# The last expert pair gets weight slots of its own, and the gate and up work of the last two pairs goes ahead of their down work

## The chip, the core and the metric

One core of a Trainium2 chip runs the whole program. The engines named here are PE (TensorE, the matrix engine), DVE (VectorE), ACT (ScalarE), POOL (GpSimd), and SP (SyncE), which does nothing but issue transfers and wait. The transfers themselves run on sixteen DMA engines. The metric is the device time of one execution in microseconds, of which each comparison takes the median of several.

## What is computed

The program is one layer of a transformer-like model for 640 tokens (512 latent ones and 128 of a prompt) of width 1024: two token mixers (retention and differential attention) with their projections, then a mixture of experts, then a final norm. All of it is float32. The change touches only the mixture of experts and the final norm:

```
# hf: the 640 normalised tokens; 4 groups of 8 experts, 32 in all
p_grp = softmax(hf @ rgw + rgb);          g_idx = top-1 group of each token
e_top, e_idx = top-2 experts in that group
w = p_top * e_top / sum(e_top)
a = silu(hf @ wg[e]) * (hf @ wu[e])       # wg, wu: 1024 x 256 of each expert
y = (a * w) @ wd[e], summed over e        # wd: 256 x 1024 of each expert
x = x + g2 * y
out = rmsnorm(x, final_norm_g)
```

Each expert has 1 MB of gate, 1 MB of up and 1 MB of down weights, 96 MB for all of them, and each is read once.

## The kernel before, in words

The 32 experts are worked through in 16 pairs (PAIRS), 0 to 15. Each expert has a block of 64 rows (tokens sent to it), and a pair fills the 128 partitions. Tokens beyond 64 for an expert would go through an overflow part that does not run on this data.

Work of one pair p, with par = p % 2:

- POOL gathers the pair's 128 token rows from DRAM into xg[par] (rows_in, L1913), and PE transposes them through PSUM banks 0 and 1 (gathered, L1037); ACT copies them to xgT[par] (L1317).
- PE multiplies them with the gate and up weights of both experts into bank 2 + par (gate_up, 16 matmuls, 32 instructions in the trace, L1043).
- ACT takes the tanh (L1322), DVE forms silu times up times the routing weight (L1779 and L1784).
- PE transposes the result into bank 4 (hidden, L1049), ACT copies it to act_aT[par] (L1326), and PE multiplies it with the down weights into banks 5 and 6 (down, L1056).
- ACT and DVE each copy half of the result to y_out[par] (L1332 and L1792), and POOL scatters the rows to y_dram in DRAM (rows_out, L1919).

PE's order is written out by hand in `pair` (L1065): gate_up of p, transpose of the rows of p + 1, hidden of p, down of p. ACT's order is in `whole`, DVE's in its own `pair`, POOL's is rows_in(p + 2) and then rows_out(p). Each engine waits on semaphores that count what the others have done: pe_gu counts finished gate_up products, pe_dn finished down products, ld_gu[slot] and ld_dn[slot] the landed weights, y_a and y_d the copied results, st_y[par] the scattered rows.

Weights live in six slots, one expert each: w_gu[0..5] and w_dn[0..5]. The first three pairs take slots 0 and 1, 2 and 3, 4 and 5. From pair 3 on only slots 0 to 3 are used, in turns: odd pairs slots 0 and 1, even pairs slots 2 and 3; slots 4 and 5 stay unused. SP refills a pair of slots in next_weights(p, e, slot): it waits until gate_up of pair p is done, issues the four gate and up loads (L652), waits until down of pair p is done, and issues the two down loads (L655). next_weights(0), (1), (3), (4), ... (13) run in this order, the last for the weights of pair 15. Between next_weights(1) and next_weights(3), behind a wait for three finished down products, SP issues three row loads for the final stage into tiles where slot 5 was: g2_rows (two, L753) and fin_row (L754), 0.5 MB each, a row of DRAM repeated to all 128 partitions.

After the last pair SP waits for all scattered rows (L762) and loads them back, five tiles of 128 tokens twice, since each token has two experts: y1[t] and y2[t] (L779 and L780). Tile 0 is summed by DVE (L1826), tiles 1 to 4 by PE, which adds both with an identity matrix into a pair of banks each (L1120 and L1121, semaphore pe_sum). DVE then does three more steps for each tile (L1831, L1832, L1834), ACT and POOL the norm, and SP the store.

## Time and profile before

| | us |
|---|---|
| median of 3 runs | 1346.71 (1345.1 to 1347.92) |
| the profiled execution, its time | 1347.75 |
| the profiled execution, its span | 1345.9 |
| granted TensorE clock over the span | 0.95 |
| busy over the span: PE | 1145.1 (85%) |
| DVE, ACT, POOL | 499.0, 402.0, 86.4 |
| DMA over the span | 222.28 MB, mean 165 GB/s |

All times on a line of the trace are microseconds from the first instruction. The expert stage begins at about 1045 and its last scatter lands at 1311.29; the rest is the read-back, the sum and the final norm. In the timeline each row is a start, a duration and an instruction; what stands in brackets is the time the engine sat idle before it and what released it. A row of a transfer on SP or POOL is its issue and not the transfer; how long that took is in the view of the DMA issues.

### The profile page before, as it was taken

Reading aid. Unit: us, or ns where it says so; the run is one execution under the profiler, and the core shown is the slowest. Engines: PE = TensorE matmul, PEld = TensorE weight load, DVE = VectorE, ACT = ScalarE, POOL = GpSimd, SP = SyncE. Lnnn points to the kernel's source line nnn. Section 1 sums busy time; section 2 is a strip of 40 time slices with the busy share of each in tenths; the row PEclk is TensorE's granted clock in tenths of the full one; section 3 lists DMA queues with packets and bytes.
Section 4 is the critical chain, followed back from the end, with each engine's and each line's share of the span. In section 5 each row is a group of like instructions: output and inputs, shape, how many; then the busy total and the mean of one; then the engine's idle time right before and its main releaser. Section 6 shows DMA issues by size and latency. Waiting matters only on the chain. (4 is left out here: it accounts for less than half of the span.)

```text
span 1345.9 us, 19161 instructions
## 1 busy us (share of the span) xinstructions
PE 1145.1 (85%) x8001; PEld 921.6 (68%) x8001; DVE 499.0 (37%) x892; ACT 402.0 (30%) x862; POOL 86.4 (6%) x103
## 2 busy tenths in 40 slices
PE   2699999999988999999988887898873888777765
PEld 0488899889987888889977776798872433222222
DVE  0521116554434344433435555546556111111115
ACT  2522222212244454542245544313120121111113
POOL 0000000211000000000000000000000111111001
PEclk9799999989999999999999999899985799999987
DMA  8655631211311312232221110924128499999925
GB/s 301 228 179 193 209 108 38 90 40 32 108 58 48 95 59 91 64 108 73 71 93 50 48 52 22 413 71 137 49 96 357 176 400 420 421 421 421 417 116 234
DMA packets 90273, 222.28 MB, mean 165 GB/s; under 512 B 9881, under 2 KB 64962, under 8 KB 74706
## 3 DMA queue, kind: packets, MB, share of 16 engines
q1 hardware_dynamic: 85586, 210.66, 42.6%
q0 software_dynamic: 4608, 10.49, 2.1%
q8 instruction: 59, 0.97, 0.3%
q14 instruction: 20, 0.16, 0.0%
HBM read 206.41 MB, written 21.00 MB: 169 GB/s over the span
## 5 line engine op out<-in xcount | busy, mean ns | idle before, releaser
L840 PE MATMUL ps<-w_high,h_high 128*128 128x256 f32 x1280 | 370.5, 289 | 10.1 <-DVE arena L1506 5.2
L840 PE MATMUL ps<-w_low,h_high 128*128 128x256 f32 x1280 | 363.9, 284 | 0.0
L840 PE MATMUL ps<-w_high,h_low 128*128 128x256 f32 x1280 | 363.7, 284 | 0.0
L840 PEld LDWEIGHTS ps<-w_high,h_high 128*128 128x128 f32 x1280 | 247.3, 193 | 24.6 <-ACT arena L1231 10.1
L840 PEld LDWEIGHTS ps<-w_low,h_high 128*128 128x128 f32 x1280 | 247.4, 193 | 0.2
L840 PEld LDWEIGHTS ps<-w_high,h_low 128*128 128x128 f32 x1280 | 247.2, 193 | 0.0
L1580 DVE TENSOR_TENSOR w_low<-w_loaded,w_high 128x2048 fp32r<-128x2048 f32 x44 | 100.8, 2291 | 174.4 <-ACT w_high L1259 174.3
L1043 PE MATMUL ps<-arena 128*64 128x512 f32 x512 | 124.1, 641 | 26.3 <-DMA arena<-in_moe_w_up 22.5
L1043 PEld LDWEIGHTS ps<-arena 128*64 128x64 f32 x512 | 40.2, 147 | 108.7 <-issue 108.7
L1231 ACT COPY arena<-ps 128x256 f32<-128x256 f32 x100 | 37.2, 372 | 249.7 <-PE ps L840 249.7
L1259 ACT CAST w_high<-w_loaded 128x2048 fp32r<-128x2048 f32 x44 | 84.0, 1908 | 57.4 <-DMA w_loaded<-in_w_o 32.9
L1286 ACT ACTIVATE arena<-ps,neg_mx 128x768 f32<-128x768 f32 (+1 forms) x80 | 62.8, 790 | 106.3 <-DVE neg_mx L1646 106.3
L1056 PE MATMUL ps<-arena 128*64 128x512 f32 x256 | 60.2, 612 | 9.8 <-ACT arena L1326 9.8
L1779 DVE SCALAR_TENSOR_TENSOR arena<-arena,ps 128x256 f32<-128x256 f32 x16 | 6.7, 421 | 145.9 <-ACT arena L1322 145.9
L1015 PE MATMUL ps<-arena 128*128 128x128 f32 x384 | 49.3, 278 | 13.3 <-ACT arena L1293 13.3
L1644 DVE TENSOR_REDUCE mx<-ps 128x1 f32<-128x768 f32 (+1 forms) x40 | 32.9, 822 | 71.5 <-PE ps L985 71.5
L1015 PEld LDWEIGHTS ps<-arena 128*128 128x128 f32 x384 | 45.5, 192 | 16.1 <-ACT arena L1293 16.1
L985 PE MATMUL ps<-arena 64*128 64x256 f32 (+2 forms) x288 | 53.9, 488 | 2.5 <-ACT arena L1180 1.5
L873 PE MATMUL ps<-const,arena 128*128 128x128 f32 x256 | 40.4, 286 | 13.2 <-POOL arena L1893 3.5
L840 PE MATMUL ps<-w_high,m_high 128*128 128x256 f32 x160 | 48.0, 300 | 2.5 <-DVE m_low L1548 0.8
L1322 ACT ACTIVATE arena<-ps 128x256 f32<-128x256 f32 x16 | 6.1, 384 | 139.2 <-PE ps L1043 139.2
L840 PE MATMUL ps<-w_high,od_high 128*128 128x256 f32 x160 | 46.2, 289 | 1.7 <-DVE od_whole L1477 0.9
(253 smaller groups left out, 1715.4 us busy)
## 6 DMA issues: line engine op xcount, KB each, us to landing
w_loaded<-in_w_in SPq DMA_DIRECT2D x32, 1024.0 KB, 5.7
arena<-in_moe_w_gate SPq DMA_DIRECT2D x32, 1024.0 KB, 13.3
arena<-in_moe_w_up SPq DMA_DIRECT2D x32, 1024.0 KB, 19.7
arena<-in_moe_w_down SPq DMA_DIRECT2D x32, 1024.0 KB, 20.9
arena<-in_w_ada SPq DMA_DIRECT2D x24, 1024.0 KB, 5.9
gates<-arena SPq DMA_DIRECT2D x40, 128.0 KB, 1.7
arena<-y_rows SPq DMA_DIRECT2D x10, 512.0 KB, 7.5
arena<-in_x_sample SPq DMA_DIRECT2D x8, 512.0 KB, 11.2
```

The costliest lines, as they stand in the source:

```text
L840: mm = pe.matmul(out[:, 0:N256], x[:, t, k * P:(k + 1) * P], w[i % 2][:, k, :], start=(k == 0 and j == 0), stop=(k == KC - 1 and j == 2))
L873: mm = pe.transpose(out[:, k * P:(k + 1) * P], src[k], ident)
L985: mm = pe.matmul(score[c][:, lo:hi], qT[h % 2][r, t * P:(t + 1) * P], keys, start=True, stop=True, skip_group_check=True)
L1015: mm = pe.matmul(pv_out, mixedT[s % 2][:, k * P:(k + 1) * P], v, start=(k == 0), stop=(k == 5))
L1043: mm = pe.matmul(B(bank_at)[BLK * i:BLK * (i + 1), :].rearrange("p (g f) -> p g f", g=2), xgT[slot][:, k, BLK * i:BLK * (i + 1)], w_gu[e0 ...
L1056: mm = pe.matmul(B(5 + n)[BLK * i:BLK * (i + 1), :], act_aT[slot][:, k, BLK * i:BLK * (i + 1)], w_dn[e0 + i][:, k, n * N512:(n + 1) * N512 ...
L1231: free(act.copy(dst[:, t, c0:c0 + N256], src), n)
L1259: act.copy(w_hi[i % 2][:], w_raw[i % 2]).then_inc(w_rounded, 1)
L1286: act.activation(probs[:, c, 0:n], score[c][:, 0:n], ACT.Exp, bias=neg_mx[:, s % 2, c:c + 1], scale=DH ** -0.5, accum_out=den[:, s % 2, c: ...
L1580: dve.tensor_tensor(w_lo[i % 2][:], w_raw[i % 2], w_hi[i % 2][:].bitcast(F32), ALU.subtract).then_inc(w_split, 1)
L1644: dve.tensor_reduce(mx[:, 0:1], score[0][:, 0:n], AXX, ALU.max)
L1779: ins = dve.scalar_tensor_tensor(out=act_s[:, par, :], in0=act_t[:, par, :], scalar=1.0, in1=src[:, 0:FF], op0=ALU.add, op1=ALU.mult)
```

## The change

SP refills slots 0 and 1 for pair 13 as before, and then issues the gate and up loads of pairs 14 and 15 together, when gate_up of pair 12 is done: pair 14 into slots 2 and 3, pair 15 into slots 4 and 5. When down of pair 12 is done it issues the four down loads of both. The three row loads of the final stage follow, behind a wait for gate_up of pair 14, and go to where slot 3 was. PE leaves its loop after pair 12, does pair 13, and then: gate_up 14, transpose of the rows of 15, hidden 14, gate_up 15, down 14, hidden 15, down 15. ACT and DVE follow this order for the last two pairs. y2 has another place, an unused tile (fin_t) is gone, and in the final sum DVE adds tiles 0 and 1 and PE tiles 2 to 4.

```diff
--- before.py
+++ after.py
@@ -198,9 +198,8 @@
         act_t, act_s = tiles(134, 2, FF), tiles(136, 2, FF)
         act_a, act_aT = tiles(194, 2, FF), [at(196 + i, 2 * P).rearrange("p (k n) -> p k n", k=2) for i in range(2)]
 
-        g2_rows, fin_row = tiles(118, 2, D), at(126, D)
-        fin_t = tiles(162, 2, D)
-        y1, y2 = tiles(28, NT, D), tiles(48, NT, D)
+        g2_rows, fin_row = tiles(138, 2, D), at(146, D)
+        y1, y2 = tiles(28, NT, D), tiles(86, NT, D)
 
         scr_at = [178]
 
@@ -747,16 +746,23 @@
 
             next_weights(0, 6, 0)
             next_weights(1, 8, 2)
-            sp.wait_ge(pe_dn, 3)
-
+            with sp.Fori(0, (PAIRS - 8) // 2) as i:
+                next_weights(2 * i + 3, 4 * i + 10, 0)
+                next_weights(2 * i + 4, 4 * i + 12, 2)
+            next_weights(PAIRS - 5, NE - 6, 0)
+
+            sp.wait_ge(pe_gu, PAIRS - 3)
+            for e, slot in ((NE - 4, 2), (NE - 3, 3), (NE - 2, 4), (NE - 1, 5)):
+                load_gate_up(e, slot)
+            sp.wait_ge(pe_dn, PAIRS - 3)
+            for e, slot in ((NE - 4, 2), (NE - 3, 3), (NE - 2, 4), (NE - 1, 5)):
+                load_down(e, slot)
+
+            sp.wait_ge(pe_gu, PAIRS - 1)
             for i in range(2):
                 sp.dma_start(g2_rows[:, i, :], mod_dram[i, 5 * D:6 * D].partition_broadcast(P)).then_inc(ld_fin, 16)
             sp.dma_start(fin_row, a["final_norm_g"].partition_broadcast(P)).then_inc(ld_fin, 16)
 
-            with sp.Fori(0, (PAIRS - 6) // 2) as i:
-                next_weights(2 * i + 3, 4 * i + 10, 0)
-                next_weights(2 * i + 4, 4 * i + 12, 2)
-            next_weights(PAIRS - 3, NE - 2, 0)
             n_over = sp.value_load(n_ov[0:1, 0:1], min_val=0, max_val=OVER)
             for par in range(2):
                 sp.wait_ge(st_y[par], 16 * PAIRS // 2)
@@ -1087,10 +1093,38 @@
             pair(0, 0, 0, 0, 0, first=True)
             pair(1, 1, 2, 0, 0)
             pair(2, 0, 4, 1, 0)
-            with pe.Fori(0, (PAIRS - 4) // 2) as i:
+            with pe.Fori(0, (PAIRS - 6) // 2) as i:
                 pair(2 * i + 3, 1, 0, i + 1, i + 1)
                 pair(2 * i + 4, 0, 2, i + 2, i + 1)
-            pair(PAIRS - 1, 1, 0, PAIRS // 2 - 1, PAIRS // 2 - 1, last=True)
+            h = PAIRS // 2 - 1
+            pair(PAIRS - 3, 1, 0, h - 1, h - 1)
+
+            a_p, b_p = PAIRS - 2, PAIRS - 1
+            for i in (2, 3):
+                pe.wait_ge(ld_gu[i], 32 * h)
+            pe.wait_ge(xt_read, a_p + 1)
+            gate_up(0, 2, 2).then_inc(pe_gu, 1)
+            pair_gathered(b_p, 1, h)
+            pe.wait_ge(gu_act, a_p + 1)
+            hidden(0).then_inc(pe_aT, 1)
+            for i in (4, 5):
+                pe.wait_ge(ld_gu[i], 64)
+            pe.wait_ge(xt_read, b_p + 1)
+            gate_up(1, 4, 3).then_inc(pe_gu, 1)
+            pe.wait_ge(aT_read, a_p + 1)
+            for i in (2, 3):
+                pe.wait_ge(ld_dn[i], 16 * h)
+            pe.wait_ge(y_a, a_p)
+            pe.wait_ge(y_d, a_p)
+            down(0, 2).then_inc(pe_dn, 1)
+            pe.wait_ge(gu_act, b_p + 1)
+            hidden(1).then_inc(pe_aT, 1)
+            pe.wait_ge(aT_read, b_p + 1)
+            for i in (4, 5):
+                pe.wait_ge(ld_dn[i], 32)
+            pe.wait_ge(y_a, b_p)
+            pe.wait_ge(y_d, b_p)
+            down(1, 4).then_inc(pe_dn, 1)
 
             n_over = pe.value_load(n_ov[0:1, 0:1], min_val=0, max_val=OVER)
             pe.wait_ge(y_a, PAIRS)
@@ -1113,12 +1147,12 @@
             with pe.Else():
                 pe.nop()
 
-            for t in range(1, NT):
+            for t in range(2, NT):
                 pe.wait_ge(ld_y[t], 32)
                 for n in range(2):
                     c = slice(n * N512, (n + 1) * N512)
-                    pe.matmul(B(2 * t - 2 + n), ident, y1[:, t, c], start=True, stop=False)
-                    mm = pe.matmul(B(2 * t - 2 + n), ident, y2[:, t, c], start=False, stop=True)
+                    pe.matmul(B(2 * t - 4 + n), ident, y1[:, t, c], start=True, stop=False)
+                    mm = pe.matmul(B(2 * t - 4 + n), ident, y2[:, t, c], start=False, stop=True)
                 mm.then_inc(pe_sum, 1)
 
         @block.scalar
@@ -1345,8 +1379,13 @@
                 for par in range(2):
                     whole(2 * i + par, par, i)
             h = PAIRS // 2 - 1
-            whole(2 * h, 0, h)
-            whole(2 * h + 1, 1, h, last=True)
+            pair_gate(2 * h, 0)
+            pair(2 * h + 1, 1)
+            pair_hidden(2 * h, 0)
+            pair_gate(2 * h + 1, 1)
+            pair_rows(2 * h, 0, h)
+            pair_hidden(2 * h + 1, 1)
+            pair_rows(2 * h + 1, 1, h)
             n_over = act.value_load(n_ov[0:1, 0:1], min_val=0, max_val=OVER)
             act.wait_ge(st_y[0], 16 * PAIRS // 2)
             act.wait_ge(st_y[1], 16 * PAIRS // 2)
@@ -1791,16 +1830,23 @@
                     dve.wait_ge(st_y[par], 16 * turn)
                 dve.tensor_copy(y_out[:, par, N512:D], B(6)).then_inc(y_d, 1)
 
-            def pair(p, par, turn, first=False):
+            def pair_act(p, par):
                 dve.wait_ge(gu_tanh, p + 1)
                 silu_up(B(2 + par), par, (gu_half, p + 1), gu_act, p)
+
+            def pair(p, par, turn, first=False):
+                pair_act(p, par)
                 pair_rows(p, par, turn, first=first)
 
             pair(0, 0, 0, first=True)
             pair(1, 1, 0, first=True)
-            with dve.Fori(1, PAIRS // 2) as i:
+            with dve.Fori(1, PAIRS // 2 - 1) as i:
                 for par in range(2):
                     pair(2 * i + par, par, i)
+            for par in range(2):
+                pair_act(PAIRS - 2 + par, par)
+            for par in range(2):
+                pair_rows(PAIRS - 2 + par, par, PAIRS // 2 - 1)
             n_over = dve.value_load(n_ov[0:1, 0:1], min_val=0, max_val=OVER)
             dve.wait_ge(st_y[0], 16 * PAIRS // 2)
             dve.wait_ge(st_y[1], 16 * PAIRS // 2)
@@ -1821,13 +1867,13 @@
 
             dve.wait_ge(ld_fin, 16 * 3)
             for t in range(NT):
-                if t == 0:
-                    dve.wait_ge(ld_y[0], 32)
-                    link(dve.tensor_tensor(y1[:, 0, :], y1[:, 0, :], y2[:, 0, :], ALU.add))
-                    both = y1[:, 0, :]
+                if t < 2:
+                    dve.wait_ge(ld_y[t], 32)
+                    link(dve.tensor_tensor(y1[:, t, :], y1[:, t, :], y2[:, t, :], ALU.add))
+                    both = y1[:, t, :]
                 else:
-                    dve.wait_ge(pe_sum, t)
-                    both = psf[:, (2 * t - 2) * N512:2 * t * N512]
+                    dve.wait_ge(pe_sum, t - 1)
+                    both = psf[:, (2 * t - 4) * N512:(2 * t - 2) * N512]
                 link(dve.tensor_tensor(y1[:, t, :], both, g2_rows[:, 1 if t == PT else 0, :], ALU.mult))
                 dve.tensor_tensor(x1[:, t, :], x1[:, t, :], y1[:, t, :], ALU.add).then_inc(x2_ready, 1)
                 dve.wait_ge(x2_ready, t + 1)
```

## Rows read from the trace of the kernel before

**Rows 1.** Page, forty slices of the span: GB/s that the DMA engines moved

```profile
GB/s 301 228 179 193 209 108 38 90 40 32 108 58 48 95 59 91 64 108 73 71 93 50 48 52 22 413 71 137 49 96 357 176 400 420 421 421 421 417 116 234
```

**Rows 2.** Windows: span, busy time by engine (instructions), PE clock, DMA share, GB/s

```profile
1099.00:1104.00 5.00, 4.73 (x26) 1.86 (x22) 0.68 (x2) 0.62 (x2) 0.80 (x1) 1.00 0.98 297
...
1124.00:1283.00 159.00, 123.03 (x558) 44.67 (x554) 17.05 (x29) 23.05 (x48) 19.24 (x19) 0.96 1.01 420
...
1283.00:1296.00 13.00, 10.05 (x40) 3.49 (x40) 0.69 (x1) 1.10 (x3) 1.00 (x1) 0.87 0.31 129
```

**Rows 3.** Chain of waits from 1200 us: start, length, what

```profile
1248.17 25.52 DMA arena<-in_moe_w_up
...
1287.32 2.49 issue
1289.80 8.80 PE ps L1043 x32
...
1308.08 3.21 DMA y_rows<-arena,to_idx
...
1312.87 6.17 DMA arena<-y_rows
```

**Rows 4.** Timeline of SP's queue: start, length, line, transfer issued

```profile
1252.90 0.81 SPq L655 DMA_DIRECT2D arena<-in_moe_w_down  x2
...
1266.96 0.53 SPq L652 DMA_DIRECT2D arena<-in_moe_w_up  x1
...
1272.33 0.80 SPq L655 DMA_DIRECT2D arena<-in_moe_w_down  x2
```

**Rows 5.** DMA issues, us to landing: loads issued at 1253.3, 1266.96 and 1272.7

```profile
arena<-in_moe_w_down SPq DMA_DIRECT2D x1, 1024.0 KB, 25.5
...
arena<-in_moe_w_up SPq DMA_DIRECT2D x1, 1024.0 KB, 22.7
...
arena<-in_moe_w_down SPq DMA_DIRECT2D x1, 1024.0 KB, 22.6
```

**Rows 6.** Timeline of PE from 1256 to 1307 us

```profile
1256.81 8.78 PE L1043 MATMUL ps<-arena 128*64 128x512 f32 x32 [3.95 <-DMA arena<-in_moe_w_up]
...
1273.92 7.09 PE L1043 MATMUL ps<-arena 128*64 128x512 f32 x32 [1.63 <-DMA arena<-in_moe_w_up]
...
1282.76 0.44 PE L1049 MATMUL ps<-const,arena 128*128 128x128 f32 x2 [0.73 <-DVE arena L1784]
...
1283.66 3.65 PE L1056 MATMUL ps<-arena 128*64 128x512 f32 x16 [0.46 <-ACT arena L1326]
...
1301.23 5.35 PE L1056 MATMUL ps<-arena 128*64 128x512 f32 x16 [0.46 <-ACT arena L1326]
```

**Rows 7.** DMA issues: loads of pair 3 (first two) and pair 5, median

```profile
arena<-in_moe_w_up SPq DMA_DIRECT2D x2, 1024.0 KB, 9.9
...
arena<-in_moe_w_down SPq DMA_DIRECT2D x2, 1024.0 KB, 11.9
...
arena<-in_moe_w_up SPq DMA_DIRECT2D x2, 1024.0 KB, 12.1
...
arena<-in_moe_w_down SPq DMA_DIRECT2D x2, 1024.0 KB, 14.5
```

**Rows 8.** Timeline of ACT, PE and DVE at the end

```profile
1306.63 0.58 ACT L1332 COPY arena<-ps 128x512 f32<-128x512 f32 x1 [5.45 <-PE ps L1056]
...
1319.08 2.07 PE L1120 MATMUL ps<-arena,const 128*128 128x512 f32 x2 [12.51 <-DMA arena<-y_rows]
...
1325.69 1.02 PE L1120 MATMUL ps<-arena,const 128*128 128x512 f32 x2
...
1325.89 1.22 DVE L1831 TENSOR_TENSOR arena<-ps,arena 128x1024 f32<-128x1024 f32 x1 [4.32 <-PE ps L1121]
```

**Rows 9.** DMA issues: fin_row load at 1096.72, and scatter of pair 13 at 1273.81

```profile
arena<-in_final_norm_g SPq DMA_DIRECT2D x1, 512.0 KB, 11.1
...
y_rows<-arena,to_idx POOLq DMA_INDIRECT x1, 8.2
```

## What the change does to the time: the prediction

> **What bounds the kernel now.** Read the page's forty slices first, then the chain of waits, then the transfers one by one, and the PE rows last. The slices of the expert stage, from the thirty-third to the thirty-eighth, all move some 420 GB/s [rows 1], and the windows say the same in another form: from 1124 to 1283 us the sixteen DMA engines are busy throughout at 420 GB/s [rows 2]. PE, which does the arithmetic, is not full there. So between 1124 and 1283 us the expert stage is a stream of weights, 6.3 MB for each of the sixteen pairs of experts, and what PE does in between is hidden. What is not hidden is the end. The chain of waits shows it [rows 3]: the second up load of pair 14 lands at 1248.17 + 25.52 = 1273.69; later the gate and up products of pair 15 run from 1289.80 for 8.80 us; the last scatter of rows starts at 1308.08 and takes 3.21 us; and the read-back of rows that PE's first sum waits for ends at 1319.04. After 1283 us the DMA engines fall idle one by one, 129 GB/s on the mean until 1296 [rows 2].
>
> Two things about the start of pair 15. The chain puts the 2.49 us ahead of it down to "issue" [rows 3], which names no releaser. The transfers do: the last up load is issued at 1266.96 [rows 4] and takes 22.7 us [rows 5], so it lands at 1289.66, and PE starts 0.14 us later. That load is what PE waits for, not the way out of the loop. Second, these products run for 8.8 us, and the same 32 instructions of pair 14 took 7.09 [rows 6]: part of them is at the lower of the two granted clocks (1.2 and 2.4 GHz); the mean of 1283 to 1296 is 0.87 [rows 2].
>
> **The change part by part.** I write times on the clock of the kernel before, and take off the shift of part 1 at the end.
>
> 1. The three row loads (1.5 MB for the final stage) go from the third pair to the end. The last of them leaves at 1096.72 [rows 9], and the window from 1099 to 1104, which holds most of their bytes, moves only 297 GB/s at a busy share of 0.98 [rows 2]. Without them the engines would be nearly empty when the weights of pair 5 are issued at about 1103, as they were when those of pair 3 were issued. The price is the difference between these two: the up loads take 12.1 us instead of 9.9, the down loads 14.5 instead of 11.9 [rows 7], so 2.2 and 2.6 us. From then on the stream has no gap, so what it gains there it keeps to its end. I take the mean, 2.4 us. The bounds are 0 (the queue would stand still for as long anyway) and 3.7 us (their whole 1.57 MB at 420 GB/s); 2.4 is nearest to the direct comparison. That PE keeps its own pace in the first pairs costs nothing, because each load of the stream is issued long before the engines come to it.
>
> 2. The gate and up loads of pair 15 are issued beside those of pair 14 and ahead of all four down loads. Nothing of the volume changes, only the order. The two down loads of pair 14 no longer lie ahead of the last up load. They are issued in one go from 1252.90 [rows 4]; the second, issued about 1253.3, takes 25.5 us [rows 5] and lands at 1278.8, and the up load ahead of it landed at 1273.69. So two down loads cost the slowest engine 5.1 us. The last up load lands at 1289.66 - 5.1 = 1284.56. Bounds: 0, if the order inside the engines is not the order of issue (a rival below), and 5.1.
>
> 3. PE does gate and up of pair 14, transposes its hidden rows, does gate and up of pair 15, and then both down products. Gate and up of pair 14 still start at 1273.92; the hidden transposes of pair 14 are over at 1282.76 + 0.44 = 1283.2 [rows 6]. PE then waits for 1284.56, so 1.4 us, and starts at about 1284.8 instead of 1289.8. Ahead of products that ran at the higher clock throughout, 1.63 us of idle time was seen; ahead of those of 8.78 us it was 3.95 and 2.49 [rows 3, 6]. 1.4 is on the side of the fast ones, so I take 7.1 us: until 1291.9. Down of pair 14 follows at once, since its weights landed at 1289.7 at the latest (now behind the last up load, 1284.56 + 5.1), and takes 3.65 us [rows 6]: 1295.55. The activation of pair 15 (ScalarE, then VectorE) is hidden beside it. Then the hidden transposes of pair 15, and 0.90 us from their start to the next down product as before [rows 6], plus ScalarE's copy of pair 14's rows, which now is ahead of the hidden copy on its queue: 0.58 us [rows 8], of which 0.4 lies beside the transposes. That makes 1.1 us; the last down product runs from 1296.65 to 1300.3. Its weights: the last down load is issued at about 1272.7 [rows 4], takes 22.6 us [rows 5] and lands at 1295.3, in either order, since the total is the same: 1.3 us to spare. Before, this point was 1301.23 + 5.35 = 1306.6 [rows 6]. That is 6.3 us: 5.0 from the earlier start, 1.7 from the clock of the gate and up products, and 0.4 lost on what is behind them (8.4 us against 8.0).
>
> 4. The row loads themselves now wait for the gate and up products of pair 14 (1281 us). Behind that wait on SP's queue is only the read-back, and it comes 30 us later. The last of the three took 11.1 us from issue to landing [rows 9], part of it behind weights. On the slowest engine they now begin behind the last down load, at 1295.3: by their bytes they are in 3.7 us later, at 1299.0, and at the worst 11.1 us later, at 1306.4. VectorE wants them only when the first rows are read back, a few microseconds behind that. The last scatter is issued 1.5 us behind the last down product (1306.6 to 1308.08), so at 1301.8. By their bytes the loads are over then, and I take nothing for it; bounds 0 and 5.0 us, the difference between a scatter on busy engines, 8.2 us [rows 9], and the last one, 3.21 [rows 3].
>
> 5. The final sum: VectorE adds tile 1 itself, and PE begins with tile 2. VectorE stood 4.32 us ahead of tile 1's product [rows 8], from 1321.57; four steps of 1.22 us now follow there, to 1326.5. PE's sum of tile 2 can start when its rows are in, 1.05 MB at 420 GB/s or 2.5 us behind tile 1's 1319.04: 1321.5. Tile 1's sum took from 1319.08 to 1325.69, 6.6 us, mostly at the lower of the two granted clocks (1.2 GHz; its first instructions take 2.07 us, and the same of the next tile 1.02 at 2.4 GHz [rows 8]). So tile 2 is ready for VectorE at 1328.3, and three tiles of three steps follow, 3.66 us each: 1339.3 instead of 1325.89 + 4 x 3.66 = 1340.5. Some of the 1.2 is lost between loads; I take 0.9. Bounds: 0, and 3.0, if PE has its full clock from the start and VectorE's 1326.5 is what counts.
>
> Other edits move nothing: the new places of the row tiles and of y2 are free when they are written, and the loops of SP, ScalarE and VectorE do the same pairs in the same order up to pair 13.
>
> Sum: 2.4 + 6.3 + 0.9 = 9.6 us. The profiled execution has a span of 1345.9 and a time of 1347.75; it would become 1338.15. It is 1.0 above the median of 1346.71, so the median becomes 1337.1.
>
> **Rivals.**
> A. The lower clock stays. If the granted clock falls in the new, shorter waits too, gate and up of pair 15 keep 8.8 us (+1.7) and one down product 5.35 instead of 3.65 us (+1.7) [rows 6]: gain 6.2, 1340.5 us. For it speaks that 1.4 us is not far from the smallest wait that had a slow group behind it (2.49); against it that 1.63 had none.
> B. Part 1 gives nothing, because the stream stands still by as much ahead of pair 5: gain 7.2, 1339.5 us.
> C. The moved rows are in the way of the last scatter, which takes 8.2 us: gain 4.6, 1342.1 us. Against it: by their bytes they are in 2.8 us before its start. For it: so few bytes were moved while they ran before [rows 2].
> D. The edit does not do what it says: the last up load lands no earlier, since the slowest engine keeps its place. Then the products of pair 15 start as now, at the lower clock, and the path behind them is 0.4 us longer: gain 2.4 - 0.4 + 0.9 = 2.9, 1343.8 us.
> E. Slower: transfers in flight share the engines. Twelve loads of 1 MB are now issued within 10 us; if they move side by side, the up loads of pair 14 come with the last of them at 1295.3 - 2.4 = 1292.9, and four products stand behind that: 9.3 us from the start of pair 14's gate and up to the end of its transposes, then 7.1, 3.65, 1.1 and 3.65, in sum 24.8, so 1317.7 against 1306.6. With the 0.9 of part 5 that is 10.2 us more, 1356.9. It decides from an arrival at 1306.6 + 0.9 - 24.8 = 1282.7, where I expect 1271.3. Against it: the up loads of pair 14 and 15 land in the order of their issue, 16.0 us apart, with 6.3 MB between them at 420 GB/s (15.0 us) [rows 3, 4, 5]; a fair share would have pulled them together.
> On E the Trainium skill has a rule: "DMA: Bandwidth & Descriptors", section "Queues, rings and completion order", says that each DMA engine takes the descriptors of one issuer's ring in order and only takes turns between rings. All these loads are SyncE's, so by that rule E gives nothing and the sum stays at 9.6; the 16.0 us above agree with it. The same section says that completion is not in order across the engines, which is what D would need.
>
> **How the numbers follow.** Chances: forecast 0.58, A 0.15, B 0.10, C 0.08, D 0.05, E 0.04. The likeliest case gives 1337.1. Its low side is all of part 1 (3.7) and part 5 (3.0) with 6.3: 13.0 us, 1333.7. A and B together give 1346.7 - 3.8 = 1342.9; the range goes up to 1342.4, which takes in A, B and C one at a time and leaves out D, E and most of the overlaps. About 2.7 us, 0.2%, is what a measurement of this kernel can tell from no change. Faster by more than that: 0.90 (forecast, A, B, C, a third of D, less the overlaps); within 0.2%: 0.06; slower: 0.04 (E).
>
> **What would show it.** Part 1: the last up load of pair 14 lands at about 1271.3 and not 1273.7, and few bytes move between 1100 and 1104. Part 2: the last up load lands 13 us behind it at most, not 16. Part 3: gate and up of pair 15 take 7.1 us, and four products follow with under 2 us of idle time between any two. Part 4: the last scatter takes about 3.2 us. Part 5: VectorE waits some 2 us ahead of tile 2 and hardly behind it. The prediction is wrong if gate and up of pair 14 start later than now, or if the last scatter is issued behind 1302 us.

## The result, and the profile after

The changed kernel takes 1339.26 us (median of 9 executions, 1335.72 to 1343.83), the kernel before 1346.14 in the same session: a ratio of 0.995, 95% interval 0.9933 to 0.9967, or 6.9 us faster. The forecast was 1337.1 us with a range of 1333.7 to 1342.4. Two more comparisons of the same pair gave 0.996 (0.9944 to 0.9976) and 0.9934 (0.9922 to 0.9947), so the gain is about 7 us (mean ratio 0.9948) where the sum said 9.6. No ratio in this document counts one execution of 2270.06 us (the changed kernel with early row loads too; its other 11 took 1337.76 to 1344.55).

The page after: span, clock granted to TensorE in forty slices (tenths), and GB/s of the DMA engines.

```profile
span 1339.0 us, 19112 instructions
...
PEclk9799999989999999999999999899985699999897
...
GB/s 304 220 173 195 211 104 53 78 57 32 103 64 47 88 63 66 86 66 111 84 91 48 32 37 40 349 123 101 117 48 343 136 398 379 422 421 422 421 271 237
```

The stream is as full as before, 421 GB/s up to the thirty-eighth slice. The last two slices differ: 271 and 237 GB/s where [rows 1] has 116 and 234. The end of the weights and the read-back have come closer together.

Windows of the kernel after: span, busy time by engine (PE, PEld, DVE, ACT, POOL), PE clock, DMA share, GB/s. In this execution the expert stage began 4.4 us later than in that of [rows 2], so the window of 1099 to 1104 us there is 1103.4 to 1108.4 here; the others stand at the same times as there.

```profile
1103.40:1108.40 5.00, 3.96 (x22) 1.63 (x18) 1.08 (x2) 1.72 (x4) 0.00 (x0) 1.00 0.53 138
...
1104.00:1124.00 20.00, 17.21 (x80) 7.22 (x78) 2.86 (x5) 4.25 (x9) 2.03 (x2) 0.91 0.89 347
1124.00:1283.00 159.00, 125.66 (x566) 46.48 (x566) 16.67 (x28) 22.35 (x46) 19.26 (x19) 0.96 1.02 421
1283.00:1296.00 13.00, 12.13 (x62) 5.22 (x60) 2.17 (x4) 2.19 (x5) 0.00 (x0) 1.00 0.74 274
```

The stretch that held the row loads before (share 0.98 at 297 GB/s [rows 2]) now has gaps, share 0.53 at 138 GB/s. The 20 us from 1104, which take in most of it, have 0.89. From 1124 to 1283 nothing has changed (1.02 at 421). Between 1283 and 1296 there are 274 GB/s where there were 129: the down loads of pair 14 and 15 and the rows now lie there.

PE at the end, as [rows 6]; in brackets the idle time before and its releaser.

```profile
1275.30 8.78 PE L1049 MATMUL ps<-arena 128*64 128x512 f32 x32 [2.04 <-issue]
...
1286.41 7.09 PE L1049 MATMUL ps<-arena 128*64 128x512 f32 x32 [0.26 <-DMA arena<-in_moe_w_up]
1293.30 3.63 PE L1062 MATMUL ps<-arena 128*64 128x512 f32 x16
1296.86 0.44 PE L1055 MATMUL ps<-const,arena 128*128 128x128 f32 x2
1297.88 3.65 PE L1062 MATMUL ps<-arena 128*64 128x512 f32 x16 [0.58 <-ACT arena L1360]
```

The gate and up products of pair 15 start 11.1 us behind those of pair 14, where [rows 6] and the chain of [rows 3] have 15.9 (1273.92 to 1289.80). They take 7.09 us, and those of pair 14 take 8.78: the other way round than before.

How the transfers came in order: SP's issues (start, length), and below them the us to landing of the up loads issued at 1251.08 and 1255.34, as [rows 4, 5].

```profile
1251.08 0.43 SPq L651 DMA_DIRECT2D arena<-in_moe_w_up  x1
1251.55 0.43 SPq L651 DMA_DIRECT2D arena<-in_moe_w_gate  x1
1252.03 1.09 SPq L651 DMA_DIRECT2D arena<-in_moe_w_up  x1
1253.16 2.14 SPq L651 DMA_DIRECT2D arena<-in_moe_w_gate  x1
1255.34 2.14 SPq L651 DMA_DIRECT2D arena<-in_moe_w_up  x1
```

```profile
arena<-in_moe_w_up SPq DMA_DIRECT2D x1, 1024.0 KB, 24.1
...
arena<-in_moe_w_up SPq DMA_DIRECT2D x1, 1024.0 KB, 31.0
```

The last up load of pair 14 lands at 1251.08 + 24.1 = 1275.2, the last one of pair 15 at 1255.34 + 31.0 = 1286.3: 11.1 us apart, 16.0 before. The chain of waits from there on (start, length, what) is as [rows 3]:

```profile
1255.34 30.98 DMA arena<-in_moe_w_up
...
1286.41 7.09 PE ps L1049 x32
...
1293.49 3.45 PE ps L1062 x16
...
1297.88 3.68 PE ps L1062 x16
...
1303.03 3.22 DMA y_rows<-arena,to_idx
...
1309.27 7.91 DMA arena<-y_rows
...
1317.23 2.08 PE ps L1154 x2
```

The last scatter takes 3.22 us, as before (3.21). Pair 15's products still wait for their last up load, and everything behind them is one unbroken chain.

VectorE in the final sum, as [rows 8]: tile 1, added by VectorE itself, and the first step on tile 2, which PE adds.

```profile
1311.70 1.23 DVE L1872 TENSOR_TENSOR arena<-arena 128x1024 f32<-128x1024 f32 x1 [9.43 <-DMA arena<-y_rows]
...
1322.64 1.23 DVE L1877 TENSOR_TENSOR arena<-ps,arena 128x1024 f32<-128x1024 f32 x1 [1.02 <-PE ps L1155]
```

It stood 4.32 us ahead of PE's first sum in [rows 8], and now 1.02.

**Two whole profiles are not a measurement.** The span fell from 1345.9 to 1339.0, which fits the medians, but by a sum of two unlike things: the part ahead of the expert pairs, which the change does not touch, came out 4.3 us longer, and the expert stage and the end 11.2 us shorter. For that reason I cut all profiles at the same events. Each row below is one profiled execution. The columns: start of the stage's first product on PE (1039.87 us in the kernel before), which ends what the expectations call the part ahead of the slot table; from the end of pair 0's gate and up products to the start of pair 14's (the stream); from there to the start of pair 15's; from there to the end of the last down product, in brackets the lengths of pair 15's gate/up and down products; from the issue of the read-back to the end; and all behind the first column (the whole stage). Between the last down product and the issue of the read-back there are always 5.0 to 5.6 us. What the stage has beyond these columns is pair 0's own gate and up products and what leads to them, 22 to 23.5 us.

| kernel | ahead | stream | 14 to 15 | 15 to last down | read-back to end | whole stage |
|---|---|---|---|---|---|---|
| before | 1039.9 | 210.6 | 15.9 | 16.8 (8.8, 5.3) | 34.4 | 306.0 |
| before, again | 1040.3 | 210.1 | 16.0 | 15.1 (8.8, 3.7) | 33.1 | 301.3 |
| after | 1044.2 | 208.8 | 11.1 | 15.1 (7.1, 3.7) | 32.5 | 294.8 |
| after, again | 1045.8 | 208.6 | 11.1 | 16.8 (8.8, 3.7) | 34.0 | 298.8 |
| after, third | 1046.1 | 208.4 | 11.1 | 16.8 (8.8, 3.7) | 32.0 | 296.7 |
| rows late only | 1039.8 | 208.8 | 16.0 | 13.4 (7.1, 3.7) | 34.9 | 300.2 |
| after, rows early too | 1041.1 | 209.8 | 11.1 | 15.1 (7.1, 3.7) | 33.6 | 297.3 |
| final sum only | 1044.1 | 210.4 | 15.9 | 15.1 (8.8, 3.7) | 32.9 | 301.5 |
| new loads, old product order | 1042.9 | 208.4 | 21.2 | 13.3 (7.0, 3.7) | 32.3 | 303.5 |
| new product order, down loads between | 1039.5 | 208.5 | 16.3 | 17.7 (9.6, 3.7) | 33.8 | 303.5 |
| after, three slot pairs | 1043.3 | 204.9 | 12.2 | 15.1 (7.1, 3.7) | 32.7 | 293.4 |
| the same, again | 1044.2 | 205.0 | 11.1 | 16.8 (8.8, 3.7) | 33.3 | 294.0 |
| before, six early row loads | 1040.2 | 215.5 | 16.0 | 15.0 (7.0, 5.3) | 35.4 | 310.2 |
| three slot pairs, old order | 1039.7 | 204.9 | 16.4 | 13.4 (7.1, 3.7) | 32.6 | 294.6 |

The columns "stream" and "14 to 15" repeat within 0.5 us for one kernel (once 1.1, in the kernel with three slot pairs). The others depend on the granted clock and don't.

### The profile page after: what moved, and what is told of

It reads as the page before. It is cut to its first block and busy times, and to the rows that moved or that the text cites. A ratio compares the mean times of both kernels' runs of the same rounds, so it can differ in the third digit from the quotient of the medians.

```text
span 1339.0 us, 19112 instructions
## 1 busy us (share of the span) xinstructions
PE 1143.7 (85%) x7993; PEld 927.6 (69%) x7993; DVE 500.3 (37%) x893; ACT 402.4 (30%) x862; POOL 88.5 (7%) x103
## 5 line engine op out<-in xcount | busy, mean ns | idle before, releaser
L846 PE MATMUL ps<-w_high,h_high 128*128 128x256 f32 x1280 | 371.2, 290 | 10.1 <-DVE arena L1545 5.2
L846 PEld LDWEIGHTS ps<-w_high,h_high 128*128 128x128 f32 x1280 | 248.0, 194 | 24.6 <-ACT arena L1265 10.1
L1293 ACT CAST w_high<-w_loaded 128x2048 fp32r<-128x2048 f32 x44 | 84.0, 1908 | 58.2 <-DMA w_loaded<-in_w_o 33.6
L1021 PE MATMUL ps<-arena 128*128 128x128 f32 x384 | 49.3, 278 | 13.3 <-ACT arena L1327 13.3
L1683 DVE TENSOR_REDUCE mx<-ps 128x1 f32<-128x768 f32 (+1 forms) x40 | 32.9, 822 | 71.5 <-PE ps L991 71.3
L846 PE MATMUL ps<-w_high,o_high 128*128 128x256 f32 x160 | 46.9, 293 | 0.8 <-DVE o_low L1587 0.8
```

Of the source, the lines that this page charges most:

```text
L846: mm = pe.matmul(out[:, 0:N256], x[:, t, k * P:(k + 1) * P], w[i % 2][:, k, :], start=(k == 0 and j == 0), stop=(k == KC - 1 and j == 2))
L1021: mm = pe.matmul(pv_out, mixedT[s % 2][:, k * P:(k + 1) * P], v, start=(k == 0), stop=(k == 5))
L1293: act.copy(w_hi[i % 2][:], w_raw[i % 2]).then_inc(w_rounded, 1)
L1683: dve.tensor_reduce(mx[:, 0:1], score[0][:, 0:n], AXX, ALU.max)
```

## The experiments

All but the second are timed against the kernel before on the same chip; the ratios have their 95% interval. They were timed in three sets, each on another chip: the pair again, part 1 alone and the changed kernel with early rows in the first; the final sum, the two halves of the new order and the three slot pairs in the second; the rest in the third. Kernels of different sets are compared by their ratios. None of them changes what is computed. The theory is the sum of the prediction; its rivals are A to E.

**The pair again.** No edit.

> The changed kernel once more. In its first profile the part from the first product of the slot table to the end of the span is 294.8 us (306.0 in the kernel before, so 11.3 less), but the part ahead of it, which the change does not touch, is 1044.2 us against 1039.9. Theory 1 (the 4.4 us ahead are chance: the granted clock of the dense part falls at other places in every execution): the part ahead lies between 1037 and 1043 here and is not tied to the kernel, and the part behind is 294 to 296 again; the ratio over five rounds is 0.992 to 0.994. Theory 2 (the changed program is slower ahead of the experts, by where its code or data lie): the part ahead is 1043 to 1045 again, and the ratio is 0.995.

> The kernel before once more, for a second look at its two parts. Theory 1 (chance): the part ahead of the slot table is anywhere from 1037 to 1044, the part behind it 305 to 307. Theory 2 (tied to the program): 1039 to 1041 again.

Measured: 0.996 (0.9944 to 0.9976), 1340.5 us against 1345.03. The profiled execution of the changed kernel took 1346.39 us, 5.9 above its own median, and that of the kernel before 1343.48. Neither theory had the numbers: the part behind the slot table is 298.8 us in the one and 301.3 in the other, the part ahead 1045.8 and 1040.3. Pair 15's gate and up products took 8.8 us in the changed kernel this time, and the last down product 3.7 in the kernel before. So both the 7.09 above and the 5.35 of [rows 6] come out otherwise in another execution of the same kernel, and the prediction had compared a good outcome with a bad one. PE in this execution of the changed kernel, pairs 14 and 15:

```profile
1277.45 7.09 PE L1049 MATMUL ps<-arena 128*64 128x512 f32 x32 [0.95 <-issue]
...
1288.56 8.78 PE L1049 MATMUL ps<-arena 128*64 128x512 f32 x32 [1.96 <-DMA arena<-in_moe_w_up]
```

Here the products of pair 14 take 7.09 us, and PE then waits 1.96 us for the last up load; above they took 8.78 us, which left a wait of 0.26.

**Part 1 alone.** The row loads of the kernel before behind its last loads of weights:

```diff
-            sp.wait_ge(pe_dn, 3)
-            for i in range(2):
-                sp.dma_start(g2_rows[:, i, :], ...)
-            sp.dma_start(fin_row, ...)
...
             next_weights(PAIRS - 3, NE - 2, 0)
+            sp.wait_ge(pe_gu, PAIRS - 1)
+            for i in range(2):
+                sp.dma_start(g2_rows[:, i, :], ...)
+            sp.dma_start(fin_row, ...)
```

> The kernel before with one edit: the three row loads are issued behind the loads of the last pair, when the gate and up products of pair 14 are done, and not in the third pair. My theory: this alone is worth the shift of the weight stream, 2.4 to 3.0 us: the part behind the slot table is 303 to 303.6 instead of 306.0, the gate and up products of pairs 8 to 14 each begin 3 us earlier against the slot table, and the last scatter is not slower (3.2 us). Rival (the weight stream stands still as long in any case): 306.0. Rival (the rows are in the way at the end): over 306.

Measured: 0.9968 (0.9953 to 0.9982), 1341.6 us. Its stream is 208.8 us, against 210.1 to 210.6. The part behind the slot table is 300.2 us, less than expected, as the last group of gate and up products came out fast. The whole change had 0.996 (0.9944 to 0.9976) in the same set: by these executions alone part 1 gained as much as all parts together (means 1341.7 and 1340.9 us, a difference of 0.8 with a 95% interval of 2.2 to either side). The window of the row loads (columns as above), and PE's last products:

```profile
1099.00:1104.00 5.00, 3.75 (x22) 1.60 (x18) 1.08 (x2) 1.83 (x4) 0.00 (x0) 1.00 0.54 139
```

```profile
1286.72 7.09 PE L1042 MATMUL ps<-arena 128*64 128x512 f32 x32 [2.57 <-issue]
...
1296.44 3.65 PE L1055 MATMUL ps<-arena 128*64 128x512 f32 x16 [0.46 <-ACT arena L1325]
```

Share 0.54, as the changed kernel's 0.53: the engines stand still for 2.3 of 5 us there, so not all that the row loads took came back. The second fence shows gate and up of pair 15 at 7.09 us behind 2.57 us of idle time. In [rows 3] they had 8.80 behind 2.49. At such a length idle time ahead of the group does not tell its clock.

**Part 1 undone in the changed kernel, and doubled in the kernel before.** Three row loads of the same kind into free space, which nothing reads; once beside the late ones of the changed kernel, once beside the early ones of the kernel before (where it makes six):

```diff
+            for i in range(2):
+                sp.dma_start(more[:, i, :], mod_dram[i, 5 * D:6 * D].partition_broadcast(P))...
+            sp.dma_start(more[:, 2, :], a["final_norm_g"].partition_broadcast(P))...
```

> The changed kernel with three row loads more, issued in the third pair as before the change, into slot 5, whose weights come much later; the late ones stay. My theory: it gives back the shift of the stream, 2.4 to 3.0 us, and nothing else: 297.2 to 297.8 us behind the slot table instead of 294.8. Rival (the shift came from somewhere else, such as the first pair's products, which ran 1.0 us faster in the first profile after): 294.8 to 295.8.

> The kernel before with three row loads more beside the early ones, into a free slot. In the other runs the products of pair 14 begin 210.1 to 210.7 us behind the end of pair 0's gate and up products with the early row loads, 208.4 to 208.9 without, so 1.8 us for 1.57 MB, where their bytes alone are 3.7 us. My theory: they lie in a gap of the weight stream (about 3.2 us idle without them), which hides the rest, and once it is full every further byte costs in full: 4 to 5.5 us more, so 214 to 216, and a ratio to the kernel before of 1.003 to 1.004. Rival (the cost of a row load is simply 0.6 us): 212.

Measured: 0.9971 (0.9957 to 0.9984), and 1.002 (1.0006 to 1.0034). The edit shown is the second's; the first differs in the place and the name. The first has a stream of 209.8 us, 1.0 to 1.4 longer than the changed kernel's, and 297.3 us behind the slot table. The second has 215.5, so the second three cost 5.1 us where the first three cost 1.8. Over whole executions (1350.21 us against 1347.22) they cost 0.2%, 2.7 us, less than the expected 0.3 to 0.4% and with an interval that ends at 4.6 us. So the 5.1 of one profile may be too much. Window of the second:

```profile
1099.00:1104.00 5.00, 4.97 (x28) 1.92 (x24) 0.43 (x2) 0.38 (x1) 1.02 (x1) 1.00 1.02 305
```

At 305 GB/s the share is 1.02: while rows move the engines are fully busy and bring less. The first three loads cost only what sticks out of a gap that is there anyway; the second three, in this profile, cost all of their time (1.57 MB at 305 GB/s is 5.2 us).

**Part 5 alone.** The kernel before with the new final sum (VectorE adds tiles 0 and 1, PE tiles 2 to 4).

```diff
-                if t == 0:
+                if t < 2:
```

> The kernel before with the final sum alone changed: VectorE adds tiles 0 and 1, PE tiles 2 to 4. My theory: from the issue of the read-back to the end of the span it takes 0.9 us less than in the kernel before (34.4 and 33.1 us in its two profiles), so 32.2 to 33.5, and VectorE waits about 2 us ahead of tile 2. Rival: nothing, because PE's first sum is as late against its rows as before and VectorE waits for it all the same: 33.1 to 34.4. Over whole runs it is near what can be measured: ratio 0.998 to 1.000.

Measured: 0.999 (0.9976 to 1.0004), not to be told from 1. VectorE ahead of its first step on tile 2:

```profile
1329.17 1.23 DVE L1831 TENSOR_TENSOR arena<-ps,arena 128x1024 f32<-128x1024 f32 x1 [1.63 <-PE ps L1121]
```

Its wait is 1.63 us and not 4.32. In the table, the stretch from read-back to end is 34.4, 33.1, 34.9 and 35.4 us with the old sum (mean 34.5) and 32.0 to 34.0 in the ten with the new one (mean 33.0). That is about 1.5 us, less than the 2 us by which either varies, so the size stays rough.

**New loads, old order of products.** The changed kernel, but PE, ACT and DVE go through pairs 14 and 15 as before:

```diff
-            gate_up(0, 2, 2).then_inc(pe_gu, 1)
...
-            down(1, 4).then_inc(pe_dn, 1)
+            pair(PAIRS - 2, 0, 2, h, h - 1)
+            pair(PAIRS - 1, 1, 4, h, 1, last=True)
```

> The changed kernel's slots and loads, but PE, ScalarE and VectorE do pairs 14 and 15 in the old order (down of 14 ahead of gate and up of 15). My theory: the early up load is wasted, since the down load of pair 14 now lands at about 248 us behind the slot table and PE waits for it ahead of the products of pair 15; these start at 251 to 252 (242.2 and 242.8 changed, 249.9 and 248.2 before) and the last down product ends at 262 to 265 (257.4 and 259.6 changed; 266.7 and 263.3 before). Rival (the loads alone are what counts): products at 246 to 247, end at 258 to 260.

Measured: 1.0029 (1.0017 to 1.0041), 1348.73 us, slower than the kernel before. PE's products of pairs 14 and 15:

```profile
1274.54 9.88 PE L1049 MATMUL ps<-arena 128*64 128x512 f32 x32 [3.69 <-issue]
...
1290.68 5.21 PE L1062 MATMUL ps<-arena 128*64 128x512 f32 x16 [4.08 <-issue]
...
1295.71 7.05 PE L1049 MATMUL ps<-arena 128*64 128x512 f32 x32
...
1305.39 3.65 PE L1062 MATMUL ps<-arena 128*64 128x512 f32 x16 [0.46 <-ACT arena L1336]
```

Down of pair 14 (1290.68) waits 4.08 us. The trace names no releaser, but its weights are the loads that were moved back: the second of them is issued at 1258.91 and lands at 1290.48, 0.2 us ahead of the product. Gate and up of pair 15 stand behind it though their own weights landed at 1285.53, and start 21.2 us behind those of pair 14. They start 252.8 us behind the slot table and the last down product ends at 266.2, both about a microsecond later than the expectation had at most.

**New order of products, down loads of pair 14 between.** The changed kernel with the slots and the early issue kept, and only the order in the stream changed:

```diff
-            for e, slot in ((NE - 4, 2), (NE - 3, 3), (NE - 2, 4), (NE - 1, 5)):
+            for e, slot in ((NE - 4, 2), (NE - 3, 3)):
                 load_gate_up(e, slot)
             sp.wait_ge(pe_dn, PAIRS - 3)
-            for ...: load_down(e, slot)
+            for e, slot in ((NE - 4, 2), (NE - 3, 3)):
+                load_down(e, slot)
+            for e, slot in ((NE - 2, 4), (NE - 1, 5)):
+                load_gate_up(e, slot)
+            for e, slot in ((NE - 2, 4), (NE - 1, 5)):
+                load_down(e, slot)
```

> The changed kernel's slots and PE order, but the down loads of pair 14 are issued between the gate and up loads of 14 and those of 15. My theory: the place in the stream is the whole gain of the loads, 2 MB or 4.8 us of it: the products of pair 15 start 15.9 us behind those of pair 14 as before, at 247, and the last down product ends at about 262 us behind the slot table. Rival (it is the early issue into free slots that counts): 11.1 us behind, at 242, and the end at 257 to 260.

Measured: 1.0011 (0.9998 to 1.0025), 1347.14 us.

```profile
1270.24 8.78 PE L1053 MATMUL ps<-arena 128*64 128x512 f32 x32 [2.04 <-issue]
...
1286.55 9.63 PE L1053 MATMUL ps<-arena 128*64 128x512 f32 x32 [5.46 <-DMA arena<-in_moe_w_up]
...
1296.01 3.61 PE L1066 MATMUL ps<-arena 128*64 128x512 f32 x16
...
1300.57 3.65 PE L1066 MATMUL ps<-arena 128*64 128x512 f32 x16 [0.58 <-ACT arena L1364]
```

From 14 to 15 it is 16.3 us again, with 5.46 us of waiting for the up load; the products of pair 15 start 247.0 us behind the slot table, as expected, and the last down product ends at 264.7, later than the 262 expected, as those products were slow. Slots of its own and an earlier issue bring pair 15 nothing; two fewer loads ahead of it bring it 5 us. And the product order without the load order gives away again what parts 1 and 5 gain, since two down products and a slow gate and up stand at the end.

**The gap filled.** The changed kernel with all six slots used in turns throughout, the loads of pair p issued when pair p - 3 has let go of its slots; the loops of SP and PE are written out:

```diff
+            for p in range(3, PAIRS - 2):
+                next_weights(p - 3, 2 * p, 2 * (p % 3))
```

and the same with the old order of loads and products for the last two pairs.

> The changed kernel with all six slots in turns from pair 3 to 15 (the loads of a pair are issued when the gate and up products of the third pair ahead of it are done), loops of SP and PE written out. My theory: the weight stream loses its one gap, ahead of pair 5, where the engines now stand 3.2 us idle in sum between 1099 and 1124 us; the products of pair 14 start 205.5 to 206.5 us behind the end of pair 0's gate and up products (208.6 and 208.8 changed, 210.1 and 210.7 before), and the ratio to the kernel before is 0.992 to 0.994. Rival (nothing left: SP stands at its full queue, or the gap only moves): 208.5 and over, 0.995 or more.

> All six slots in turns and the late row loads, but the old order of loads and products for the last two pairs. My theory: it keeps the stream's gain (products of pair 14 at 205 us behind the end of pair 0's gate and up products), but pair 15 follows 16 us behind 14, and not 12; the last down product ends 4 to 5 us later than with the new order (255.5 behind the slot table), at 260. Rival (with more loads in flight the order no longer counts): 255 to 256.

Measured: 0.9932 (0.9915 to 0.995), 1336.86 us, and 0.9954 (0.9937 to 0.9971), 1340.38 us. Windows of the first:

```profile
1099.00:1104.00 5.00, 5.00 (x26) 1.63 (x24) 0.69 (x1) 0.58 (x1) 2.02 (x2) 1.00 1.01 426
1104.00:1124.00 20.00, 17.61 (x90) 6.74 (x88) 2.86 (x5) 4.25 (x9) 2.02 (x2) 1.00 1.02 420
1124.00:1270.00 146.00, 115.43 (x530) 43.41 (x526) 16.68 (x28) 22.32 (x46) 18.98 (x19) 0.96 1.02 421
```

Share 1.01 from 1099 on, 426 GB/s: no gap, and a stream of 204.9 us, 3.7 less than the changed kernel's 208.6. With these slots the new order of loads and products is worth 0.22%, some 3 us, by two sets, with intervals that overlap. The stage shows only 1.2 (293.4 against 294.6): 4.2 less from 14 to 15, 1.7 more behind it, where the new order has its second down product, and the rest where neither kernel differs. That was less than the 4 to 5 us expected, and the first sign of what part 3 really costs.

**Once more, side by side.**

> The changed kernel a third time, beside the next one. Part behind the slot table 294 to 299 us, products of pair 15 11.1 us behind those of pair 14, part ahead of the slot table between 1039 and 1046 as in all kernels (chance). Ratio to the kernel before 0.995 to 0.996.

> The changed kernel with all six slots in turns, again, on the same chip as the changed kernel: 3 to 3.5 us faster than it in the median (my theory: the gap of 3.2 us in the stream is closed), ratio to the kernel before 0.992 to 0.994. Rival (the first result was chance): equal to the changed kernel.

Measured: the changed kernel 0.9934 (0.9922 to 0.9947), 1338.29 us; the three slot pairs 0.9913 (0.9898 to 0.9927), 1336.93 us. The version with three slot pairs is the fastest here, each time some 0.2% ahead of the changed kernel (0.9932 to 0.995, 0.9913 to 0.9934). In this last comparison the two intervals still overlap from 0.9922 to 0.9927, so its lead over the changed kernel is likely and not more (1.4 us by the medians, where 3 to 3.5 were expected); over the kernel before it is 0.7 to 0.9%. The three slot pairs with the old order of loads and products were timed beside these two on the same chip. There the new order is worth 0.4%: 0.9913 (0.9898 to 0.9927) against 0.9954 (0.9937 to 0.9971), 3.5 us by the medians, with intervals that do not meet, from four executions of each.

## Why the prediction was right, and where its sum was too large

The measured median lies in the range, 2.2 us above the forecast. The sum against the table's means:

| part | forecast, us | measured, us | from |
|---|---|---|---|
| 1, stream | -2.4 | -1.8 | 210.35 to 208.6 |
| 2, pair 15 earlier | -5.0 | -4.8 | 15.9 to 11.1 |
| 3, clock, and what is behind pair 15 | -1.3 | +1.2 | 14.8 to 16.0 |
| 4, late rows | 0 | 0 | 3.22 |
| 5, final sum | -0.9 | -1.5 | 34.5 to 33.0 |
| sum | -9.6 | -6.9 | whole kernel: -7.0 |

**Part 1: right mechanism, a little too large.** Row loads move at 297 to 305 GB/s with the engines fully busy, and the stream kept what it lost to them. That is not rival B: part 1 alone gave 0.9968. (That is 4.3 us, with an interval from 2.4 to 6.3, more than the 1.8 of the stream; what the rest is no run shows.) The step that was mis-sized is "from then on the stream has no gap": where the rows were, a gap opens without them (share 0.54 in the one kernel, 0.53 in the other), and only what stuck out of it was to be had. The up and down loads of [rows 7] measured the delay of single loads, which is not the whole stream's.

**Part 2: right, and by the profiles the core of the gain.** 4.8 us against 5.0; the last up load landed 11.1 us behind that of pair 14, where at most 13 was the sign. It landed at 1286.3 and not at 1284.6 because the part ahead of the stage was 4.3 us longer, pair 0 1.0 shorter, and part 1 took 1.8 off. The experiment with the down loads between (16.3 us with all else kept, ratio 1.0011 against 0.9948) shows that the place in the stream did it. D (the slowest engine keeps its place) and E (loads in flight share the engines) are false: with eight gate and up loads issued within 8 us the up loads still landed in order and 11.1 us apart. (Issuing all twelve took SP 21 us and not the 10 of rival E, as told below. Gate loads can't be read this way: gate and up of a slot count on one semaphore, so the view can give a gate load a landing that is too early.) By bytes two down loads less between them are 2.1 MB at 421 GB/s, 5.0 us, and 4.8 came. The rule that each engine takes one issuer's descriptors in order (Trainium skill, "DMA: Bandwidth & Descriptors", section "Queues, rings and completion order") agrees with these 11.1 us.

**Part 3: the step that failed.** The prediction took 7.1 us for pair 15's gate and up products, since the wait ahead of them would be short, and 3.65 for the last down product, and held this against 8.80 and 5.35 in the one profile of before. Neither price belongs to an order of work. The last down product took 5.35 us in two of the fourteen profiles, both with the old order, and 3.65 in all others. Gate and up of pair 15 took 8.8, 8.8, 8.8, 7.1, 7.0 and 7.1 us in the six profiles with the old order of loads and products, and 7.1, 8.8, 8.8, 7.1, 7.1, 8.8 and 9.6 in the seven with the new order of products.

What the prediction read about the wait holds in part. Pairs 1 to 15 of all fourteen profiles have 210 groups of these 32 instructions. All 127 with at most 1.89 us of idle time ahead took 7.0 to 7.1 us; of the 36 with 1.92 to 3.06, 19 took longer; of the 47 with more, 42 did (8.4 to 10.1 us). The forecast of the wait was what fell short: 1.4 us to the landing, or 1.6 to the first product. Of the six profiles with the new order of loads and products four have pair 14's products at 7.09 us, as the sum assumed: PE then stood 1.92 to 1.98 us, and three of these four groups took 8.78 us. In two they took 8.78 or 9.94 us: PE stood 0.22 or 0.26 us, and both groups behind took 7.09. So the wait behind a pair 14 of 7.09 us came just into the stretch where both lengths occur, and which of them comes there no row looked at here tells (2.57 us had 7.09 behind it, 2.49 had 8.80).

At equal clocks (7.1 and 3.7) the stretch is 13.4 us in the old order and 15.1 in the new, 1.7 more, because two down products and the hidden transposes stand behind pair 15's gate and up instead of one down product. The prediction priced this at 0.4 because it gave the old order the slow down product. On the mean (16.8, 15.1, 15.1, 13.4, 15.0 and 13.4 with the old order; 15.1, 16.8, 16.8, 15.1, 15.1 and 16.8 with the new order of loads and products) it is 1.2 us. So of the 6.3 us of parts 2 and 3, 3.6 are left. Rival A was half right: in two of the three profiles of the changed kernel the clock did fall in the wait ahead of pair 15, but not in each, and the last down product was never the slow one there.

**Parts 2 and 3 need each other.** Loads alone made the kernel 0.29% slower, product order alone 0.11% slower (its interval just takes in no change), each with parts 1 and 5 in it, and together they are about half of a gain of 0.5%. In the kernel with the loads alone PE's queue is blocked by a down product whose weights were sent behind.

**Part 4: right.** C is false: the last scatter took 3.22 us in the chain, and the last row load had landed at 1300.80, 2.2 us ahead of it. The late row loads cost nothing that the trace shows.

**Part 5: right sign.** VectorE's wait fell from 4.32 us to 1.02 and 1.63; the whole stretch says 1.5 us, the kernel with this edit alone 0.999 with 1 in its interval.

**The signs of being wrong.** The prediction named two, and by the clock of the profile both came: gate and up of pair 14 started at 1275.30, later than 1273.92, and the last scatter was issued at 1303.03, behind 1302. They had left out that the part ahead of the stage can move. Counted from the stage's first product (1039.9 and 1044.2 us) the products start at 231.1 instead of 234.1, and the scatter goes at 258.8 where the sign was 262.1. So what the signs were meant to catch did not happen.

**What stays open.** How the gain splits among the parts rests on profiles of single executions. Timed executions alone bear it out in part: in the first set part 1 alone had 0.9968 and the whole change 0.996, which leaves 0.8 us (give or take 2.2) for parts 2, 3 and 5, where the table has 5.1; in the third, with three slot pairs, the new order alone was worth 3.5 us. The part ahead of the expert pairs took 1039.5 to 1046.1 us in these profiles, in code that the change does not touch; all three profiles of the changed kernel have it long (1044.2 to 1046.1) and both of the kernel before short. It is not the program alone: profiled executions in which it took over 1043 us lie above their kernel's median (by 1.6, 5.9 and 6.3 us for the changed kernel, 1.7 and 3.1 with three slot pairs, 2.8 with the final sum alone), and those with under 1042 from 4.2 below to 1.0 above in all but one case (2.0, with the six row loads). The measured gain of 7.0 us agrees with the stage's 6.9 without it. Whether a microsecond of it belongs to the program is not settled.

## What to carry to other kernels

Where a stream of loads is the bound, its end is too: put last in the stream what has the least work behind it, and give the engine that uses it the same order, since either edit alone brought no gain here. Price an added or moved load by what sticks out of the gaps around it, at its own rate (a row repeated to 128 partitions came at some 300 GB/s of 421). Before a term of a sum is taken from the length of one group of matmuls, see whether a second execution of the same kernel has the same length. And place windows by an event of the trace and not by its clock, since here the stage began up to 6.6 us later in one profile than in another.

## What the hardware showed beside that

- SP's issue of a 1 MB load took 0.43 us up to a point, then 1.09 and 2.14 us each, as the rows of SP's queue above show; the four down loads took it 13.34 us in all. It began with about ten 1 MB loads in flight. So SP was held back at about the pace of the stream (1 MB at 421 GB/s is 2.5 us). Nothing was lost here, as the engines stayed full; in the kernel with three slot pairs SP was held like this through the stage, and it was the fastest. But anything queued on SP behind such loads would start later; this was not tried.
- One and the same group of 32 instructions took 7.1, 8.8 or 9.6 us from execution to execution, as its granted clock differed: over the 7.09 us of pair 15 in the first profile of the changed kernel it was 1.00, over the 8.78 us in the second 0.81, over the 9.63 us with the down loads between 0.73. With at most 1.89 us of idle time ahead it was never slow (127 groups); with 1.92 to 3.06 it was slow in 19 of 36, and no row looked at here tells which.
